# Hybrid DeltaNet and Conformer step: one half block read, some taps, GpSimd's sums and a LayerNorm step take other places

## The reference

```python
proj = h @ w_in                      # q, k, v | beta, decay | z | GLU input | gates a, b
qkv = silu(causal_dwconv(qkv_pre, conv_qkv_w))            # 4 taps
o, s_new = gated_delta_chunked(q, k, v, g, beta, s0)      # a triangular solve a chunk, then the recurrence
glu = glu_in[..., :CONF_WIDTH] * sigmoid(glu_in[..., CONF_WIDTH:])
c = causal_dwconv(conf_ext, conf_dw_w) + conf_dw_b        # 31 taps
o_b = silu(layernorm(c, conf_ln_g, conf_ln_b))            # over all 1024 channels
mixed = sigmoid(gate_a) * o_a + sigmoid(gate_b) * o_b
x = x + rmsnorm(mixed @ w_out); y = x + rmsnorm(relu(rmsnorm(x) @ w_up)**2 @ w_down)
```

## Time and profile before

| | us |
|---|---|
| median of three runs | 1057.67 (1057.59 to 1058.25) |
| the profiled execution | 1057.45 |
| its span in the trace | 1055.7 |
| PE busy | 1038.3 (98%) |
| DVE, ACT, POOL busy | 745.4, 592.1, 634.6 |

### The profile page before, as it was taken

The page is one execution under the profiler, slowest core; times in us unless marked ns, Lnnn a source line. Parts: engine busy times, 40 slices in busy tenths (PEclk is TensorE's granted clock), DMA queues, the critical chain, the costliest instruction groups (busy, mean ns, idle before and its releaser), DMA issues.

```text
span 1055.7 us, 21847 instructions
## 1 busy us (share of the span) xinstructions
PE 1038.3 (98%) x7971; PEld 1012.8 (96%) x7971; DVE 745.4 (71%) x1254; ACT 592.1 (56%) x1105; POOL 634.6 (60%) x546
## 2 busy tenths in 40 slices
PE   8999999999999999999999999999999999999997
PEld 6999989999999999999999999999999999999997
DVE  7989898898888988889867757594544444444335
ACT  7855556575565755656646865765444443343632
POOL 1894686684876948768583443646555555555631
PEclk9999999999999999999999999999999999999999
DMA  6312212222122221322222162122222223222402
GB/s 239 105 68 81 95 42 92 84 80 95 40 91 84 79 95 40 93 81 90 88 77 61 43 250 80 41 70 97 98 96 81 81 83 114 82 79 79 116 7 89
DMA packets 32651, 92.08 MB, mean 87 GB/s; under 512 B 4688, under 2 KB 12240, under 8 KB 32592
## 3 DMA queue, kind: packets, MB, share of 16 engines
q1 hardware_dynamic: 32592, 91.29, 26.2%
HBM read 82.76 MB, written 8.52 MB: 86 GB/s over the span
## 4 chain that ended last, share of the span: by engine, by line
PE 80%; DVE 7%; POOL 4%; issue 3%; ACT 2%; DVEq 0%; ACTq 0%; POOLq 0%
PE ps L749 26%; PE ps L1162 15%; PE ps L1110 13%; PE ps L758 7%; PE ps L1194 5%; PE ps L714 3%; DVE ps L1908 3%; DVE t_r L1905 1%; PE ps L1006 1%; POOL in_lo L2601 1%; DVE work L2139 1%; PE ps L768 1%; POOL work L2601 1%; POOL w_lo L2601 1%; POOL o_a L2601 1%
## 5 line engine op out<-in xcount | busy, mean ns | idle before, releaser
L2601 POOL TENSOR_TENSOR w_lo<-raw,w_hi 128x1024 fp32r<-128x1024 f32 x100 | 241.2, 2414 | 157.0 <-ACT w_hi L1734 50.2
L749 PE MATMUL ps<-in_hi,w_hi 128*128 128x288 f32 x944 | 286.1, 303 | 1.1 <-ACT work L1408 0.6
L749 PE MATMUL ps<-in_lo,w_hi 128*128 128x288 f32 x944 | 282.3, 300 | 0.7 <-POOL in_lo L2601 0.7
L749 PE MATMUL ps<-in_hi,w_lo 128*128 128x288 f32 x944 | 282.7, 300 | 0.0
L1908 DVE SCALAR_TENSOR_TENSOR ps<-work,ct,ps 128x512 f32<-128x512 f32 x240 | 180.5, 752 | 7.1 <-DVE work L2068 1.6
L749 PEld LDWEIGHTS ps<-in_hi,w_hi 128*128 128x128 f32 x944 | 177.7, 188 | 2.7 <-issue 1.2
L749 PEld LDWEIGHTS ps<-in_lo,w_hi 128*128 128x128 f32 x944 | 177.3, 188 | 1.0 <-POOL in_lo L2601 0.9
L749 PEld LDWEIGHTS ps<-in_hi,w_lo 128*128 128x128 f32 x944 | 177.6, 188 | 0.5
L1905 DVE TENSOR_TENSOR o_a<-o_a,ps 128x576 f32<-128x576 f32 (+1 forms) x63 | 42.8, 681 | 107.3 <-PE ps L1162 73.1
L2601 POOL TENSOR_TENSOR w_lo<-t_pair,w_hi 128x1024 fp32r<-128x1024 f32 x18 | 43.6, 2422 | 42.5 <-ACT w_hi L1763 29.7
L1291 ACT CAST w_hi<-raw 128x1024 fp32r<-128x1024 f32 x63 | 65.6, 1043 | 0.2
(11 more groups left out here) (396 smaller groups left out, 2862.3 us busy)
## 6 DMA issues: line engine op xcount, KB each, us to landing
raw<-w_all_in SPq DMA_DIRECT2D x135, 512.0 KB, 3.7
work<-s_in_in SPq DMA_DIRECT2D x8, 512.0 KB, 3.4
s_sample_out<-work SPq DMA_DIRECT2D x8, 512.0 KB, 2.6
xt<-x_t_in SPq DMA_DIRECT2D x4, 576.0 KB, 6.4
xt<-x_t_in SPq DMA_DIRECT2D x2, 1152.0 KB, 7.1
y_out<-o_a SPq DMA_DIRECT2D x14, 144.0 KB, 1.9
halo<-halos_in SPq DMA_DIRECT2D x9, 156.0 KB, 3.5
conf_rows_out<-c_rows SPq DMA_DIRECT2D x8, 135.0 KB, 3.4
```

The lines of the kernel that those rows point to most:

```text
L749: t = mm(dense_ps(n, j, h), a[:, w, k], b[:, k, h * HALF:(h + 1) * HALF], start=r == 0, stop=r == PASS_MM // 2 - 1)
L2601: return gp.tensor_tensor(out, a, b, op)
```

## The change

- ACT, passes 1 to 7: in slot 18 the read of the first half block comes behind the level-seven copies, and the pass's other slots stay. In pass 1 the bias read and tap copy move from slot 24 to 25.
- ACT, pass 8: the squares of the LayerNorm (slots 15 to 18) come behind the level's copies.
- DVE: taps are shared out otherwise over the slots. In all passes one tap more is left to the `early` part, or moved inside it.
- POOL and DVE: POOL adds the first 15 of the 31 products to the second 15, in place, and DVE reduces the last 16 of them. `conv31_p` now counts to four a pass.
- DVE, pass 8: `head(n, s)` comes first in slots 14 to 19, ahead of the subtraction and the sums of squares; the scaling of slots 22 to 25 stays ahead of it.

```diff
--- before.py
+++ after.py
@@ -1432,7 +1432,7 @@
                   scale=hc[0:SMP, 5 * BETA + 4:5 * BETA + 5]).then_inc(us_ready, 1)
 
             def phase(n):
-                for s in range(33):
+                def read_first(s):
                     pos, j = evac_first(n, s)
                     if pos is not None and not (last(n) and pos == 7):
                         act.wait_ge(job_done, 2 * (base(n) + pos) + 1)
@@ -1445,6 +1445,10 @@
                         if j >= Q:
                             act.wait_ge(qrows_ready, 3 * n - 2 + j - Q)
                         half_read(n, pos, j, 0)
+
+                for s in range(33):
+                    if last(n) or s != 18:
+                        read_first(s)
                     pos, j = evac(n, s)
                     if pos is not None and not (last(n) and pos in (7, 9)):
                         act.wait_ge(job_done, 2 * (base(n) + pos) + 2)
@@ -1458,7 +1462,7 @@
                         conv_silu(n, conv_slots(n, 2).index(s))
                     if n_is(n, 1) and s == 1:
                         conv_silu(0, 2)
-                    if s == (11 if last(n) else 24 if n_is(n, 1) else 19):
+                    if s == (11 if last(n) else 25 if n_is(n, 1) else 19):
 
                         act.wait_ge(conv31_done, n)
                         dst = conf[:, n - 1] if isinstance(n, int) else \
@@ -1473,11 +1477,6 @@
                     if last(n) and s == 14:
                         act.wait_ge(mu_ps, 1)
                         A(job_ps(1), job_ps(1), ACT.Copy, scale=1.0 / D).then_inc(mu_ready, 1)
-                    if last(n) and 15 <= s < 19:
-
-                        for k in (2 * s - 30, 2 * s - 29):
-                            act.wait_ge(xc_ready, k + 1)
-                            A(xc_squares(k), conf[:, k], ACT.Square).then_inc(xc_sq, 1)
                     if last(n) and s == 21:
                         log_exp()
                         act.wait_ge(var_ps, 1)
@@ -1522,6 +1521,13 @@
                             A(uc_r[:, 0:SEQ // 2], uc_t, ACT.Copy).then_inc(uc_ready, 1)
                         if s == 8 and not last(n):
                             conv_silu(n, 0)
+                    if s == 18 and not last(n):
+                        read_first(s)
+                    if last(n) and 15 <= s < 19:
+
+                        for k in (2 * s - 30, 2 * s - 29):
+                            act.wait_ge(xc_ready, k + 1)
+                            A(xc_squares(k), conf[:, k], ACT.Square).then_inc(xc_sq, 1)
                     if s == 22:
 
                         act.wait_ge(kd_ps, n)
@@ -2032,8 +2038,9 @@
 
                 n_ = NS // 2
                 at = SEQ + half * n_ * LS
-                dve.wait_ge(conv31_p, 2 * h + half + 1)
-                ve.tensor_reduce(v["c31"][:, at:at + n_ * LS].rearrange("p (s a) -> p s a", s=n_), conf_products(),
+                dve.wait_ge(conv31_p, 4 * h + 2 * half + 2)
+                ve.tensor_reduce(v["c31"][:, at:at + n_ * LS].rearrange("p (s a) -> p s a", s=n_),
+                                 conf_products()[:, :, :, CF_TAPS // 2:CF_TAPS],
                                  mybir.AxisListType.X, ALU.add).then_inc(conv31_s, 1)
 
             def qkv_conv(n, i, a, b):
@@ -2183,14 +2190,14 @@
                     dve.wait_ge(zs_ready, n + 1)
                     stt(o, v["db"], pcol("delta_g", 0), v["zs"], ALU.mult, ALU.mult).then_inc(head_out, 1)
 
-            early = {1: 4, 2: 1, 3: 2, 8: 1, 14: 1, 16: 1}
-            early_1 = {1: 3, 2: 2, 3: 2, 8: 1, 10: 1, 12: 1, 14: 1, 16: 1, 21: 5, 22: 2, 23: 2}
-            early_2 = {1: 4, 2: 2, 3: 2, 8: 2, 9: 1, 10: 1, 12: 1, 14: 1, 16: 1, 18: 2}
-            early_3 = {1: 4, 2: 1, 3: 2, 8: 2, 12: 1, 14: 1, 16: 1}
-            early_8 = {1: 3, 2: 1, 4: 1, 6: 2, 7: 1, 8: 1, 9: 1}
-            late = {21: 3, 22: 2, 23: 2, 24: 4, 25: 2, 26: 2, 27: 1, 28: 1, 29: 1, 30: 2, 31: 1}
-            late_1 = {25: 3, 26: 3, 27: 2, 28: 1, 29: 1, 30: 3, 31: 1}
-            late_2 = {21: 2, 22: 2, 23: 2, 24: 3, 25: 2, 26: 2, 27: 1, 28: 1, 29: 1, 30: 2, 31: 1}
+            early = {1: 4, 2: 1, 3: 2, 8: 2, 14: 1, 16: 1}
+            early_1 = {1: 3, 2: 1, 3: 2, 8: 1, 12: 1, 14: 1, 16: 2, 21: 5, 22: 3, 23: 2}
+            early_2 = {1: 4, 2: 1, 3: 2, 8: 2, 9: 1, 12: 1, 14: 1, 16: 2, 18: 3}
+            early_3 = {1: 4, 2: 1, 3: 2, 8: 2, 12: 1, 14: 1, 16: 1, 18: 2}
+            early_8 = {1: 3, 2: 1, 4: 1, 6: 2, 7: 1, 8: 1, 9: 2}
+            late = {21: 3, 22: 2, 23: 2, 24: 3, 25: 2, 26: 2, 27: 1, 28: 1, 29: 1, 30: 2, 31: 1}
+            late_1 = {25: 3, 26: 3, 27: 2, 28: 1, 29: 2, 30: 2, 31: 1}
+            late_2 = {21: 2, 22: 2, 23: 2, 24: 3, 25: 2, 26: 1, 27: 1, 28: 1, 29: 1, 30: 1, 31: 1}
 
             def convolutions(n, s):
                 proj = not last(n)
@@ -2235,6 +2242,15 @@
 
             def phase(n):
                 for s in range(32):
+                    if last(n) and 22 <= s < 26:
+
+                        for k in (2 * s - 44, 2 * s - 43):
+                            if k == 0:
+                                dve.wait_ge(ln_scale, 2)
+                            tt(two(conf[:, k]), two(conf[:, k]), job_ps(1), ALU.mult).then_inc(ln_scaled, 1)
+                    if n_is(n, 1) and s == 0:
+                        dve.wait_ge(in_ready, KB)
+                    head(n, s)
                     if last(n) and 14 <= s < 18:
                         for k in (2 * s - 28, 2 * s - 27):
                             if k == 0:
@@ -2244,15 +2260,6 @@
                         k = 2 * s - 32
                         dve.wait_ge(xc_sq, k + 2)
                         tt(xc_squares(k), xc_squares(k), xc_squares(k + 1), ALU.add).then_inc(xc_pair, 1)
-                    if last(n) and 22 <= s < 26:
-
-                        for k in (2 * s - 44, 2 * s - 43):
-                            if k == 0:
-                                dve.wait_ge(ln_scale, 2)
-                            tt(two(conf[:, k]), two(conf[:, k]), job_ps(1), ALU.mult).then_inc(ln_scaled, 1)
-                    if n_is(n, 1) and s == 0:
-                        dve.wait_ge(in_ready, KB)
-                    head(n, s)
                     if not n_is(n, 1) and s == 0:
                         head_cols(n)
                     if n_is(n, 1) and s == 0:
@@ -2795,6 +2802,10 @@
                         tt(conf_products(), windows(v["gext"], GXT, GXS, half * n_, n_, CF_TAPS),
                            ct[:, 0:CF_TAPS].unsqueeze(1).unsqueeze(1).to_broadcast([P, n_, LS, CF_TAPS]),
                            ALU.mult).then_inc(conv31_p, 1)
+                        pool.wait_ge(conv31_p, 4 * n - 3 + 2 * half)
+                        m_ = CF_TAPS // 2
+                        tt(conf_products()[:, :, :, m_:2 * m_], conf_products()[:, :, :, m_:2 * m_],
+                           conf_products()[:, :, :, 0:m_], ALU.add).then_inc(conv31_p, 1)
                     if s == 19:
 
                         pool.wait_ge(t_ready, LEVELS * n)
```

## The result

The changed kernel takes **1073.58 us** (median of four runs, 1071.91 to 1075.67) against 1057.84 for the kernel before beside it: ratio 1.0149, 95% interval 1.0127 to 1.0172: slower by 1.5%. The forecast was 1066.0 with a range up to 1069.5. The direction was right; 7.6 us are missing in the size.

What follows compares the result with a forecast made beforehand. The prediction took TensorE, busy 98% at full clock, to bound the kernel. 7.2 (passes 3 to 7) + 1.3 (passes 1 and 2) - 0.2 (pass 8) = +8.3 on 1057.67 gave 1066.0 us, range 1061.5 to 1069.5.

Steps and rivals of the forecast that it cites:

- What bounds the kernel: Whole kernel: PE busy 98%, clock full, so time is gained or lost only where PE stands still.
- the sum: All terms added, 7.2 + 1.3 - 0.2 = +8.3 us, giving 1066.0 us.
- Part 1: Slot 18's half read behind the copies: table load delays matmul 241, +1.45 us a pass, +7.2 in passes 3 to 7.
- The Trainium skill's drain: Table switch: about 1380 ns beyond the load, some 9 us more over seven passes; set aside for the rows.
- (a): Rival, passes 1 to 7: the table load comes ahead of the copies, saving 9.0 us: 1057.0 us; chance 5%.
- (b): Rival, slot 19: matmul 241 does not wait for the moved read, copies' 0.44 us won: 1053.0 us; chance 5%.
- Part 4: Passes 1 and 2, moved taps and later bias read: together +1.3 us, bounds -1.2 and +3.5.
- Its series: Pass 1: bias read behind GpSimd's gates and the square, no longer beside them; first tap at 110.9, 3.0 us later.
- Part 2: Halved sums on GpSimd and VectorE: cost nothing in passes 1 to 7, +0.6 us at slot 10 of pass 8.
- Part 3: Pass 8's new order: level-seven difference comes earlier, L918 waits less; -0.8 us, bounds -1.3 to -0.4.
- Pass 8 together -0.2: Pass 8: halving's loss of 0.6 us and the new order's gain of 0.8 us, net -0.2 us.

Runs made afterwards that it cites:

- experiment 2: Kernel before with only the half read of slot 18 moved behind the level-seven copies in passes 1 to 7: 1073.24 us, ratio 1.0144.
- experiment 3: Changed kernel with the Sigmoid's table loaded explicitly ahead of slot 18's copies in passes 1 to 7, the read still behind them: 1063.17 us, ratio 1.0042.
- experiment 4: Changed kernel with 13 useless matmuls ahead of job 5's first matmul, so PE works instead of waiting: 1070.01 us, ratio 1.0114.
- experiment 10: Kernel before with the half read behind the copies, its table load ahead of them, one dense matmul moved from slot 19 to 20: 1056.21 us, ratio 0.9986.
- experiment 8: Changed kernel with 6 useless matmuls ahead of job 5's first matmul, shortening PE's stop there: 1069.14 us, ratio 1.0107.
- experiment 11: Kernel before with only the change's tap tables, bias read in slot 24: 1057.95 us, ratio 1.0007.
- experiment 9: Changed kernel with a second table load behind slot 18's copies in passes 1 to 7, lengthening PE's stop: 1089.7 us, ratio 1.0304.
- experiment 12: Kernel of experiment 10 plus the tap tables (bias read in slot 24, no halving) and pass 8's new order for slots 16 to 19: 1057.95 us, ratio 1.0005.

## Why the prediction was right in direction and wrong in size

**What bounds the kernel.** The reading of the rows was right, and its conclusion, that time "is lost only where it is made to" stand still, was the failure. A stop has a second price: the clock behind it. The forecast put seven stops of 1.6 to 1.8 us and one of 3 us more on PE and took from "the granted clock is full in all 40 slices" that it stays full. **The step that failed is the sum: it had no term for the clock.** The kernel before has no stop of that length in its passes (its longest at these lines are 0.7, 0.3 and 1.2 us). Outside them it has one of 1.8 us at the very start and one of 1.59 us at L1226 near the end, and behind the latter the clock of its profile stayed full. One such case is no proof of a price of zero: the same 1.59 us is followed by a half-clock stretch in 5 of the 14 profiles of this case. The price should have been bounded from both sides. Five stretches at 0.50 of 3.4 us cost about 1.6 us each, together 7.9 of the 17.6 us between the two profiled runs; in the medians, 15.7 us apart, the other terms leave about 6. The Trainium skill has the mechanism (TensorE: Matmul & The Clock Gate, "HAM oscillation — how this bites in real kernels": a stop in each turn of a loop lets the clock fall in each turn, and one pays half of the throttled time). The windows agree: 17 to 19 matmuls in 3.4 us instead of 31, and the falls come with the stops of the loop. They differ in two things, and there the measurement decides: the fall does not come with each stop, and where the Trainium skill's example stops for a DMA wait of some 3 to 5 us, 1.65 us was enough here.

**Part 1** was right in every link: the waits of 1.65 us, the load behind u_r, 1.35 us in pass 6 after against 1.45, 7.27 with the clock out of it against 7.2. That is shown by experiments 2, 3 and 4. The Trainium skill's drain, by which the prediction would have been higher (an estimate: seven of 1.38 us are 9.7, not some 9), is seen nowhere in these rows. Rivals (a) and (b) are out: the load is not placed ahead by itself, and matmul 241 stands on the read. Their conditions made true by hand did save time: (a)'s in experiment 3 gave 10.4 us against the kernel after, clock included; (b)'s was tried only together with (a)'s, in experiment 10, which came to 1056.2 where (b) had 1053.0.

**Part 4** was right in its size. At the end of pass 2 the kernel is 4.4 us behind, 3.1 of them two stretches, which leaves 1.3, the forecast. Its series is confirmed with the read's stretch out of the way (experiment 8: 3.1 us at L980 against 3.0); in the kernel after the first tap came at 112.4 instead of 110.9 because that stretch stands ahead of it. What it had not seen is that pass 2 would gain through taps and halving together, as its taps alone do not, and that the taps cost up to 1.3 us in pass 3 (experiment 11), of which 0.3 shows behind the longer wait.

**Part 2** was right in its durations and in slot 10 of pass 8 (0.66 against 0.6), and wrong in "costs nothing in passes 1 to 7": it looked at the idle time ahead of the second product and not at what is queued behind it on GpSimd. In the kernel after these 0.25 us are hidden in the longer wait (a pass at full clock costs 1.35, against 1.45 for part 1 alone), so that they hardly moved the total.

**Part 3** was right at L918 (-0.78 against -0.8) and wrong about the end of the pass: VectorE's work ahead of x_last did not get less, it only stands in another order, and L953 gives back 1.2. "Pass 8 together -0.2" measured **+1.3**: 1.5 us, the second missing term. The prediction followed the moved steps to the first thing that they had held, and not to the next.

**The sum again**, with what was measured: 7.2 (passes 3 to 7, three stretches of 1.6 taken off) + 1.3 (passes 1 and 2, two taken off) + 1.3 (pass 8) + 7.9 for the clock = 17.7, with rounding the 17.6 of the table. Without the clock the forecast of 8.3 would have been short by 1.4, all of it in pass 8.

**Still open** is why the clock falls behind one 1.65 us wait and not behind the next one like it. Experiments 4, 8 and 9 show that the stop is what it takes, and that the longer it is the more often and the longer the clock falls (seven of 0.9 us: never; seven of 1.65 to 1.74: four, and five in experiment 2 (1.65 to 1.75); seven of 2.94 to 3.03: six). The other stops of the 14 profiles fit in, the first of each kernel aside: behind none of the other 28 between 0.85 and 1.52 us did the clock fall, behind the 1.59 us of L1226 in 5 of 14, behind the seven of 2.07 to 2.08 us every time. They do not show what decides in a single case: experiment 11's 1.65 us at L915 and one of 1.75 us near the start of experiment 12 had no fall, and the passes in which it comes differ between the kernel after and experiment 2. There is one trace of each kernel.

## What to carry to other kernels

Price a new stop of TensorE of about 1.6 us or more twice, its own length and a possible 1.6 us of fallen clock behind it (up to 3 us behind one of 2.9), and keep the second as an upper bound where the trace of before has no stop of that length. Before an instruction is moved behind another, look at what it brings along (here a table load) and at every later reader of its semaphore, by counting positions in the queue: the load and one matmul's place together decided here between +1.4 us a pass and -0.26. And when an engine works without a gap up to a due result, changing the order ahead of that result moved the wait in pass 8 but did not remove it.

## What the runs showed of the hardware

The granted clock fell to half behind stops that were much shorter than I had thought to matter: four times in seven at 1.65 us, never in seven at 0.9 us. It came back by itself after 3.4 us, in some cases after 6.8. Matmuls that compute nothing of use, put into the stop, kept the clock up and made the kernel 3.6 us faster than without them. In single stretches the lower clock cost less than half of its length where PE waited in it anyway: the stretch of experiment 9 from 381.8 has PE busy for only 5.77 of 6.80 us, and its pass is 2.6 us longer than pass 7 of the same run, where the clock stays full. A table load that was asked for ahead of time ran beside PE's work without any cost that the trace shows, and the Sigmoid behind it needed no second one, although two other operations stand between (experiment 3).
